# Down weights of a mixture-of-experts layer loaded in two 2 MB transfers in place of four of 1 MB

## The reference

```python
# moe_ffn: h has 512 rows of 1024; 32 experts, each token goes to 4 of them
logits = hf @ w_router + b_router
top_logits, top_idx = lax.top_k(logits, 4);  top_w = softmax(top_logits)
...                       # the rows are grouped by expert
gu   = xb @ w_gate_up[e] + b_gate_up[e]           # w_gate_up[e]: 1024 x 2048, 8 MB
gate = minimum(gu[:, ::2], 7.0);  up = clip(gu[:, 1::2], -7.0, 7.0)
act  = (up + 1.0) * (gate * sigmoid(gate * 1.702))
ys   = act @ w_down[e] + b_down[e]                # w_down[e]: 1024 x 1024, 4 MB
y    = segment_sum(ys * weight, token)
```

## Time and profile before

| | us |
|---|---|
| median of 3 runs | 2026.53 |
| lowest, highest | 2023.01, 2026.72 |
| profiled execution, its own time | 2022.45 |
| its span, first to last instruction | 2020.6 |
| TensorE busy | 1942.9 (96%) |
| VectorE busy | 543.9 (27%) |
| ScalarE busy | 310.8 (15%) |
| GpSimd busy | 195.0 (10%) |

### The profile page before, as it was taken

One profiled execution on the slowest core, in us unless ns is written; L12 is line 12 of the kernel. 1 busy time (PEld: TensorE's weight loads), 2 busy tenths in 40 slices (PEclk: granted clock), 3 DMA queues, 4 the chain that ended last, 5 costly groups with the idle time before them and its releaser, 6 DMA issues.

```text
span 2020.6 us, 41366 instructions
## 1 busy us (share of the span) xinstructions
PE 1942.9 (96%) x17698; PEld 890.8 (44%) x17698; DVE 543.9 (27%) x986; ACT 310.8 (15%) x598; POOL 195.0 (10%) x243
## 2 busy tenths in 40 slices
PE   6999989999999999997999999999999999999995
PEld 5445555555455444443343444434343434343332
DVE  0272553553623121044121111111121212111116
ACT  3132323413322100021000000000000000000002
POOL 0001010010010000012011101010101111110101
PEclk8999999999999999998999999999999999999996
DMA  9111111111101422337999999999999999999985
GB/s 377 48 63 48 42 42 48 43 37 32 42 22 42 151 86 86 114 121 277 366 408 398 402 400 401 402 394 406 393 406 386 411 388 403 395 398 390 402 338 214
DMA packets 80602, 496.34 MB, mean 246 GB/s; under 512 B 13735, under 2 KB 14267, under 8 KB 26608
## 3 DMA queue, kind: packets, MB, share of 16 engines
q1 hardware_dynamic: 71936, 478.82, 60.7%
q0 software_dynamic: 8592, 16.48, 2.5%
HBM read 478.00 MB, written 25.64 MB: 249 GB/s over the span
## 4 chain that ended last, share of the span: by engine, by line
PE 82%; DMA 10%; DVE 4%; issue 1%; DVEq 1%; ACT 1%; SPq 0%; ACTq 0%
PE ps L1063 33%; PE ps L570 21%; PE ps L565 13%; DMA arena<-bias_parts 10%; PE ps L1078 8%; PE ps L778 2%; DVE arena L1461 2%; PE ps L1058 1%; DVE arena L1464 1%; PE ps L890 1%; PE ps L885 1%; PE ps L1041 1%; PE ps L1048 1%; PE ps L865 0%; PE ps L659 0%
## 5 line engine op out<-in xcount | busy, mean ns | idle before, releaser
L1063 PE MATMUL ps<-arena 128*32 128x512 f32 x6144 | 667.0, 593 | 0.0
L1063 PEld LDWEIGHTS ps<-arena 128*32 128x32 f32 x6144 | 191.7, 110 | 454.7 <-issue 448.6
L570 PE MATMUL ps<-hT,arena 128*128 128x512 f32 x768 | 351.9, 601 | 7.9 <-DVE arena L1461 7.9
L1078 PE MATMUL ps<-arena,hT 128*32 128x256 f32 x6144 | 338.1, 380 | 1.1 <-ACT hT L1127 1.1
L1078 PEld LDWEIGHTS ps<-arena,hT 128*32 128x32 f32 x6144 | 198.5, 110 | 129.9 <-ACT hT L1127 1.6
L1127 ACT ACTIVATE arena<-ps 128x512 f32<-128x512 f32 (+4 forms) x148 | 88.5, 598 | 848.7 <-PE ps L1048 656.7
L570 PEld LDWEIGHTS ps<-hT,arena 128*128 128x128 f32 x768 | 140.2, 192 | 154.6 <-issue 149.4
L1979 DVE TENSOR_SCALAR arena<-ps 128x768 f32<-128x768 f32 x32 | 30.6, 958 | 650.1 <-PE ps L1063 650.1
L2098 POOL DMA_INDIRECT expert_rows<-hT,six x96 | 96.9, 1010 | 782.0 <-ACT hT L1127 761.3
L570 PE MATMUL ps<-arena 128*128 128x512 f32 x256 | 118.5, 604 | 2.2 <-DVE arena L1461 2.2
L1990 DVE STREAM_TRANSPOSE hT<-arena 128x768 f32<-128x768 f32 x32 | 31.3, 978 | 208.2 <-PE ps L1078 208.1
(11 more groups left out here) (229 smaller groups left out, 1190.0 us busy)
## 6 DMA issues: line engine op xcount, KB each, us to landing
arena<-in_w_gu SPq DMA_DIRECT2D x256, 1024.0 KB, 11.0
arena<-in_w_dn SPq DMA_DIRECT2D x128, 1024.0 KB
arena<-in_w_pair SPq DMA_DIRECT2D x16, 1024.0 KB, 5.0
arena<-in_w_merge SPq DMA_DIRECT2D x16, 1024.0 KB, 4.9
expert_rows<-oaT SPq DMA_DIRECT2D x4, 2048.0 KB, 26.5
arena<-expert_rows SPq DMA_DIRECT2D x16, 512.0 KB, 6.2
arena<-in_x SPq DMA_DIRECT2D x8, 512.0 KB, 6.4
arena<-in_w_qb SPq DMA_DIRECT2D x4, 768.0 KB, 4.3
```

The lines of the kernel that those rows point to most:

```text
L570: ins = pe.matmul(region(name)[:, cols], lhsT, rhs, start=(k == 0), stop=(k == n - 1))
L1063: ins = pe.matmul(gu[32 * j:32 * (j + 1), g, :], xT[:, k, 32 * g:32 * (g + 1)], ring[k][:, 512 * j:512 * (j + 1)], start=False, stop=(k == ...
L1078: ins = pe.matmul(yd[32 * j:32 * (j + 1), g, 0:256], aT[:, g, 2 * c + k, :], ring[8 + c][:, D * k + 256 * j:D * k + 256 * (j + 1)], start= ...
```

## The change

The down weights of an expert are loaded by two transfers of 2 MB. The first fills the buffers at 4 and 6 of the arena, the second those at 12 and 14, now seen as two buffers of 16 KB per partition. Each takes 16 KB per partition in one run. A transfer is issued when the second of its two halves has been used by the expert before. TensorE waits on `chunk_in[8]` ahead of its first two down steps and on `chunk_in[10]` ahead of the last two. The order of SP's queue, the bytes, the places in SBUF and all arithmetic stay.

```diff
         ring = [ar(a, 2 * K1) for a in (8, 10, 16, 18, 20, 22, 0, 2, 4, 6, 12, 14)]
+        down_ring = [ar(a, 4 * K1) for a in (4, 12)]
...
         def w_dn_chunk(e, c):
-            kk = c - 8
-            return w_dn[bass.ds(e, 1)].rearrange("o (p r) f -> p (o r) f", p=P)[:, 2 * kk:2 * kk + 2, :].rearrange("p r f -> p (r f)")
+            kk = (c - 8) // 2
+            return w_dn[bass.ds(e, 1)].rearrange("o (p r) f -> p (o r) f", p=P)[:, 4 * kk:4 * kk + 4, :].rearrange("p r f -> p (r f)")
...
             def down_weights(n, e):
-                for c in range(8, 12):
+                for c in (8, 10):
                     if not first(n):
-                        sp.wait_ge(dn_used, 4 * n + (c - 7 - 4))
-                    sp.dma_start(ring[c], w_dn_chunk(e, c)).then_inc(chunk_in[c], 16)
+                        sp.wait_ge(dn_used, 4 * n + (c - 6 - 4))
+                    sp.dma_start(down_ring[(c - 8) // 2], w_dn_chunk(e, c)).then_inc(chunk_in[c], 16)
...
                 for c in range(4):
-                    pe.wait_ge(chunk_in[8 + c], 16 * n + 16)
+                    pe.wait_ge(chunk_in[8 + c - c % 2], 16 * n + 16)
```

## The result

The changed kernel takes 2028.01 us (median of 20 runs, 2024.56 to 2031.62), the kernel before 2023.38 (20 runs, 2020.65 to 2030.31). The ratio is 1.0022 with a 95% interval of 1.0014 to 1.003: the change makes the kernel slower by 4.6 us. I had forecast 2.7 us less. What came is the second rival, which had put 4.6 us on it.

The account below looks back on a forecast made before the run. TensorE, then from about 1337 us the DMA queue through the late bias, was taken to bound the kernel. Packets -5.8, later issue +2.6 and tail +0.5 gave -2.7 us: 2023.8 us from a 2026.53 median, range 2016 to 2032.

Parts of the forecast that it names:

- the second rival: Down weight loads: the idle hole behind the up loads costs more than the packets save; +4.6 us, 2031.1 us, chance 0.27.
- What bounds the kernel: Expert stage: TensorE first, then the DMA queue through the late bias transfer; 10.2 us of loss from expert 2 to 31.
- Packets, -5.8 us: Down weights in the DMA queue: 16 KB packets in place of 8 KB save 0.2 us per expert, 29 times.
- a later pace of 32.85 us per expert: Sign of a right forecast: the pace of the experts once the chain of waits has turned to the bias transfer.
- The 0.2 us per expert: DMA work saved by 16 KB runs, from 38.5 against 37.7 engine-us per MB in two windows of q1.
- Later issue, +2.6 us, once: First down transfer issued one step later: the DMA idle hole near expert 2 grows by 2.6 us, once.
- Gather and scatter: Gathers behind 16 KB packets may take 2 us longer, which 5 us of cover before TensorE's use hide.
- Tail, +0.5 us: Expert 31's down weights land later and meet the scatter's packets; 0.5 us, between 0 and 2.5.
- The rule weighed: Larger transfers run nearer peak, with about 2 us fixed cost each; halving the transfers would lift the DMA limit; minority chance.
- Chances: Odds given for the whole change: faster 0.33, same 0.43, slower 0.24, with about 0.2% as the limit of same.

Follow-up runs that it names:

- moving the bias: Kernel before, with the 12 KB bias transfer issued right behind the first up chunk instead of the eighth: 2006.0 us, ratio 0.9918.
- the changed kernel with the early bias: Changed kernel, with the bias transfer issued right behind the first up chunk instead of the eighth: 2012.9 us, ratio 0.9951.
- one, one, two: Kernel before, with only the third and fourth down transfers merged into one of 2 MB, issued when the fourth was: 2024.9 us, ratio 1.0006.
- late pairs: Kernel before, four 1 MB down transfers issued in pairs at the changed times: 2033.9 and 2033.8 us; with another row group order 2028.1 us.
- the larger pause: Changed kernel, with both 2 MB transfers issued only after all four down steps of the expert before: 2065.1 us, ratio 1.021.

## Why the prediction was wrong

*What bounds the kernel:* right, and shown by moving the bias. Its worth was put too low: 17.0 us came back where the middle holds 10.2, the rest mostly before expert 2, where TensorE's wait of 5.1 us for the bias of expert 1 goes as well. The profiles hold 13.7 us of the 17.0 (spans of 2020.6 and 2006.9). I had also written that the granted clock is full in all of the expert stage; it is so from expert 2 on, but 0.92 between 923 and 990 us, with 10.2 us at the lower of its two levels from 949 us on, around TensorE's wait for that bias, which ends at 955 us. In the changed kernel with the early bias it is 1.00 from 920 to 988 us.

*Packets, -5.8 us:* **the term that failed.** Against the kernel before, the 16 KB runs save nothing: over 600 us of full queue the two run lengths need 40.3 and 40.4 engine-us per MB (40.2 and 40.6 in the second profiles). My sign for it was a later pace of 32.85 us per expert; between experts 13 and 31 it is 33.13 and 33.27 in the changed kernel, 33.08 and 33.15 before. With half of the down weights in 16 KB runs and the first issues at their old times (one, one, two) the time does not fall either. The 0.2 us per expert came from two windows that differ in traffic and not only in run length. The packet records show it: the window at 669 to 675 us also has 25 packets of 8 KB, and they take 309 ns each, where those at 1336 to 1347 take 314 in the mean and those of 1300 to 1900 take 329. Like for like, in one window, two 8 KB packets take 618 ns and one of 16 KB takes 611, so 7 ns, or 0.11 us per expert: half of my term, and just the value at which the second rival begins. The queue's share, 90% there, is not what matters: in 670 to 674 us it is 103.1% with 1.77 MB, 37.3 engine-us per MB. The trace allowed the test that I did not make, to compare both sizes inside one window, and then to ask whether 7 ns outlast a busy queue.

One comparison stands beside this. At equal issue times and in the changed kernel's own row order, merging the pairs took 5.9 us off (2033.9 to 2028.0), as if the packet term were right and the later issue cost 10.3. The windows of 600 us, the pace and one, one, two speak against that reading, but it is not excluded that the longer run undoes a cost that only late pairs in this order have.

*Later issue, +2.6 us, once:* right in place and kind, and in size up to expert 13. The strip shows 2.7 us of standstill, the loss up to expert 13 grows by 2.6 us, the bias binds from expert 9 or before where it was expert 13, no pause no loss (one, one, two), and the larger pause costs every expert what was worked out for it in the mean. The term has nothing for the further 1.7 us behind expert 13, nor for the 10.3 us of late pairs in the old row order. With the packet term at zero my sum would have read +2.6 + 0.5 = +3.1 us, or 0.15%.

*Gather and scatter:* right, TensorE waits for no gather, and they land after 9.3 us in the median, 9.7 at most.

*Tail, +0.5 us:* too small in the profiles, 2.5 us on the mean of the two pairs. I had 7.5 us for a lone 2 MB load, and the first took 7.4 (1974.0 to 1981.4). The second, beside the scatter, took 9.7 (1979.2 to 1988.8), and the third set of rows waited behind all that.

*The rule weighed,* that of the Trainium skill ("DMA: Bandwidth & Descriptors", section Bandwidth) by which larger transfers run nearer to the peak: its table is of transfers that GpSimd issues, and these are issued by SP. The runs here bear it out at best in part. At one run length and row order, two transfers in place of four took 2027.2 against 2028.1 us, and eight in place of four 2030.0 against 2033.3, not more. Only the late pairs in the old row order gain by the merge, 5.9 us, and there the run length changed with it.

*Chances:* the second rival had 0.27, and slower 0.24. The saving that decides it, 0.11 us per expert, was worked out there; against the kernel before, the measured saving is under it. That its number fits to a tenth is partly luck: it is 2.6 for the hole and 2 for the tail, and the profiles show 4.3 in the middle and 2.5 in the tail where the medians show 4.6.

## What to carry to other kernels

When many loads share one queue that is nearly full, ask of a merged load first when its issue moves, and whether the queue has work until then: the 2.6 us lost here at expert 2 were not won back by expert 13. Put a small transfer that is needed first ahead of the large ones that are needed later; here 12 KB in the right place were worth 17 us. Compare the cost of packets of two sizes inside one window, or between windows with the same traffic beside them; an equal share of the queue is not enough. And look whether an edit that changes the run length also changes which rows are read.

## What the runs showed that I had not expected

Late pairs of 1 MB cost +10.3 and +11.6 us, or +4.5 us, by the order in which the row groups of the down weights are read, at equal bytes, packets and issue times (2033.9 and 2033.8 against 2028.1). With the bias early and the queue never dry, late pairs in the old order grow by 0.50 us per expert, hardly more than the 0.46 of the unchanged transfers. What in the memory or the queue makes this difference stays open.

With an early bias the queue falls behind by 0.46 us in every expert, to 19.4 us from issue to landing at 1870 us, and up to expert 31 TensorE never waits for a weight: the ring holds enough of them for one stage of this length. Only the last down part waits, 1.6 us with the unchanged transfers and 4.5 us with the 2 MB ones.

A load has landed when all of its 16 parts have, and one part falls behind the others. In the kernel before, the last part of an up chunk lands at most 2 us behind the fifteenth up to expert 9, and 2 to 5 us behind it in most of the last ten experts (the seven up chunks whose 16 landings the trace has whole). A load so waits for one late engine, and the shares and idle times above are means over all 16; they can't show what that one engine loses.
